# Feed-forward stages: every piece of modulation rows at the end of its group

## The reference

```python
def ada_chunks(s, w, b, k):
    mod = s @ w[:, :k * D_MODEL] + b[:k * D_MODEL]
    return [m[:, None, :] for m in jnp.split(mod, k, axis=-1)]

def swiglu(h, w_gate, w_up, w_down):
    return (jax.nn.silu(h @ w_gate) * (h @ w_up)) @ w_down

h = x + g2 * swiglu(rms_norm(x) * (1 + sc2) + sh2, ...)   # in outline, layer by layer
```

## Time and profile before

| | |
|---|---|
| runs (us) | 2203.38, 2204.43, 2203.44; median 2203.44 |
| profiled execution | 2204.52 us, of which the span from the first to the last instruction is 2202.7 us |
| mean granted TensorE clock | 0.996 |
| busy | PE 2156.7, DVE 1847.5, ACT 1327.0, POOL 112.2 us |
| stage 0 of the feed-forward stages | from 201.75 us to about 397 us |
| stage 1 | from 531 to 725 us |
| stage 2 | from 857 to 1052 us |

### The profile page before, as it was taken

One profiled execution on the slowest core, in us unless ns is written; L12 is line 12 of the kernel. 1 busy time (PEld: TensorE's weight loads), 2 busy tenths in 40 slices (PEclk: granted clock), 3 DMA queues, 4 the chain that ended last, 5 costly groups with the idle time before them and its releaser, 6 DMA issues.

```text
span 2202.7 us, 31747 instructions
## 1 busy us (share of the span) xinstructions
PE 2156.7 (98%) x12960; PEld 1899.7 (86%) x12960; DVE 1847.5 (84%) x2321; ACT 1327.0 (60%) x1495; POOL 112.2 (5%) x155
## 2 busy tenths in 40 slices
PE   6999999999999999999999999999999999999998
PEld 4888999889999979999888888888888888888886
DVE  7967888876998677888896988989897988989896
ACT  3574433575343776434633777777777777777775
POOL 3000111000010000100000000000000000000021
PEclk9999999999999999999999999999999999999999
DMA  9855988625887616885643899999998999999992
GB/s 370 299 190 201 344 314 316 230 77 211 305 299 276 225 39 239 325 325 179 227 171 136 325 372 370 365 345 363 370 358 343 369 365 371 368 345 357 373 360 85
DMA packets 137360, 633.30 MB, mean 288 GB/s; under 512 B 9304, under 2 KB 21625, under 8 KB 115194
## 3 DMA queue, kind: packets, MB, share of 16 engines
q1 hardware_dynamic: 112698, 536.83, 64.9%
q0 software_dynamic: 24512, 94.38, 11.4%
HBM read 630.13 MB, written 1.05 MB: 287 GB/s over the span
## 4 chain that ended last, share of the span: by engine, by line
PE 82%; DVE 12%; DMA 3%; issue 2%; ACT 1%; SPq 0%; DVEq 0%; ACTq 0%
PE ps L1266 80%; DVE wring_rounded L3211 3%; DMA aring<-in_ada_rows 3%; DVE aring L3238 2%; DVE work L3211 1%; PE ps L2391 1%; DVE OT L3235 1%; PE ps L1469 1%; DVE F L3218 1%; DVE F L3211 0%; PE ps L1444 0%; DVE work L3750 0%; ACT scr_rounded L2472 0%; ACT F_rounded L2472 0%; DVE work_rounded L3211 0%
## 5 line engine op out<-in xcount | busy, mean ns | idle before, releaser
L3211 DVE TENSOR_TENSOR wring_rounded<-wring,scr_rounded 128x2048 fp32r<-128x2048 f32 (+1 forms) x314 | 569.6, 1845 | 58.2 <-ACT scr_rounded L2472 57.8
L2472 ACT ACTIVATE scr_rounded<-wring 128x2048 fp32r<-128x2048 f32 (+1 forms) x314 | 479.7, 1553 | 181.8 <-PE ps L1266 125.3
L1266 PE MATMUL ps<-wring_rounded,OT_rounded 128*128 128x512 f32 (+1 forms) x1184 | 314.8, 390 | 2.6 <-DVE wring_rounded L3211 1.7
L1266 PEld LDWEIGHTS ps<-wring_rounded,OT_rounded 128*128 128x128 f32 x1184 | 220.1, 188 | 47.2 <-DVE wring_rounded L3211 2.3
L3238 DVE CUSTOM_DVE_ANT_0 aring<-aring,F,vec 128x1024 f32<-128x1024 f32 x152 | 187.9, 1283 | 35.6 <-DMA aring<-in_ada_rows 34.8
L3211 DVE TENSOR_TENSOR wring_rounded<-wring,H_rounded 128x2048 fp32r<-128x2048 f32 (+1 forms) x85 | 193.9, 2281 | 24.2 <-ACT H_rounded L2472 24.0
L3211 DVE TENSOR_TENSOR wring_rounded<-wring,aring_rounded 128x2048 fp32r<-128x2048 f32 x84 | 193.4, 2302 | 12.4 <-ACT aring_rounded L2472 12.1
L2472 ACT ACTIVATE H_rounded<-wring 128x2048 fp32r<-128x2048 f32 (+1 forms) x85 | 162.3, 1910 | 54.7 <-issue 38.4
L2472 ACT ACTIVATE aring_rounded<-wring 128x2048 fp32r<-128x2048 f32 x84 | 161.2, 1919 | 54.4 <-PE ps L1266 54.4
L1266 PE MATMUL ps<-V_rounded,wring_rounded 128*128 128x256 f32 x1184 | 177.9, 285 | 4.6 <-DVE wring_rounded L3211 4.6
L1266 PE MATMUL ps<-work_rounded,F_rounded 128*128 128x256 f32 x1056 | 169.8, 283 | 0.0
(11 more groups left out here) (391 smaller groups left out, 3695.8 us busy)
## 6 DMA issues: line engine op xcount, KB each, us to landing
wring<-in_moe_gate SPq DMA_DIRECT2D x56, 2048.0 KB, 8.5
wring<-in_moe_up SPq DMA_DIRECT2D x56, 2048.0 KB, 9.0
wring<-in_moe_down SPq DMA_DIRECT2D x56, 2048.0 KB, 8.6
aring<-in_ada_rows POOLq DMA_DIRECT2D x88, 1024.0 KB, 7.5
wring<-in_ffn_w_gate SPq DMA_DIRECT2D x10, 2048.0 KB, 11.0
wring<-in_ffn_w_up SPq DMA_DIRECT2D x10, 2048.0 KB, 15.3
wring<-in_ffn_w_down SPq DMA_DIRECT2D x10, 2048.0 KB, 10.5
wring<-in_diff_w_in SPq DMA_DIRECT2D x6, 2048.0 KB, 15.3
```

The lines of the kernel that those rows point to most:

```text
L1266: return pe.matmul(dst, lhsT, rhs, start=start, stop=stop, **kw)
L2472: return act.activation(dst, src, ACT.Copy, **kw)
L3211: return ve.tensor_tensor(dst, x, y, op)
```

## The change

In VectorE's group the conditional piece between the gate remainders and the down remainder is taken out, and all of the group's pieces are made at its end, behind the remainders of weights and activations. The number of pieces of every group, and their order among themselves, stay.

```diff
                 for n in range(FG):
                     if n + 1 < FG:
                         ff_lower_parts(f, L, n + 1, "g")
-                    if PIECES[f][n] == 3:
-                        piece()
                     ve.wait_ge(down_upper_made, FG * f + n + 1)
                     tt(down_weights(L, n), down_weights(L, n, False), down_upper(n).bitcast(F32),
                        ALU.subtract).then_inc(down_lower_made, 1)
@@
-                    for _ in range(min(PIECES[f][n], 2)):
+                    for _ in range(PIECES[f][n]):
                         piece()
```

## The result

The changed kernel takes **2210.77 us** (median of 8 runs, 2209.41 to 2212.36), the kernel before 2203.57 us on the same chip (8 runs, 2203.21 to 2205.24): a ratio of 1.003, 95% interval 1.0021 to 1.0039. It is slower by 7.2 us. The forecast was 2214.6 us, slower by 11.2: right in direction and mechanism; three of its terms were too large, and it missed a fourth.

A forecast was written before the change was run, and what follows sets the result against it. The prediction took the kernel to be bound by TensorE's matmuls. Stage 0 7.2, stage 1 2.0, stage 2 0 and clock 2.0 sum to +11.2 us on 2203.4: 2214.6 us, range 2201 to 2223.

The forecast's parts named there:

- What bounds the kernel: Whole kernel: bound by its matmuls, TensorE busy 98% of the span; time moves only where TensorE waits or stops waiting.
- part 2: Groups with three pieces in a row: VectorE needs 13.26 us plus a refill, against TensorE's 17.28 us a group.
- L: Refill time of the third piece's buffer, from GpSimd's issue to use of the rows; read as 5.46 to 10.98 us.
- part 1: Stage 0: up-remainder waits and a wait at 273.90 us can go, gaining 4.3 us at most.
- part 3: Stage 0, groups 4 to 7: four refills sum to 30.6 us, pair 9 effectively starts at 364.1 us, +7.2 us.
- part 6: Lower clock behind the last late pair of a stage: 0 to 2.0 us a stage, 2.0 us taken once.
- part 4: Stage 1, three moved groups at the median refill: pair 10 starts at 704.5 us instead of 702.57, +2.0 us.
- part 5: Stage 2: two moved pieces stand alone and could bear a refill of 12.8 us, so 0.
- The signs: Timeline: third pieces wait 3 to 8 us; TensorE waits for first gate remainders of pairs 6 to 9 in stage 0.
- The lead covers it: Rival: refills get shorter, stage 0 comes out even at 5.9 us each; 2202 to 2207 us, chance 0.20.
- Order is what hurt: Rival: the up remainder is free, 4.3 us come back, nothing new is late; 2199.1 us, chance 0.05.
- Every third refill is a slow one: Rival: weight loads and rows collide each time, clock falls in both stages; 2222 to 2230 us, chance 0.13.

The follow-up runs named there:

- The buffer experiments: Third ring buffer in stage 0 against the kernel before: old order 2200.86 us, with stage 0's five pieces moved 2200.42 us; before 2203.21 us.
- the runs above: Kernels moving only stage 1's three pieces (2205.69 us) or only stage 2's two (2204.28 us), against the kernel before, 2203.59 us.
- the kernel with stage 1 alone: Only the three pieces of stage 1 (groups 6 to 8) moved, against the kernel before: 2205.69 us against 2203.59, ratio 1.001.
- the kernel with stage 0 alone: Only the five pieces of stage 0 (groups 3 to 7) moved, against the kernel before: 2208.51 us against 2203.59, ratio 1.0023.
- the kernels with stage 2 and stage 1 alone: Only stage 2's two pieces moved, 2204.28 us; only stage 1's three moved, 2205.69 us; each against the kernel before, 2203.59 us.
- groups 6 and 7 of stage 1: Only these two groups' pieces moved, group 8 as before, against the kernel before: 2205.26 us against 2203.59, ratio 1.0007.
- three buffers: Third ring buffer for the rows in stage 0, old order, against the kernel before: 2200.86 us against 2203.21, ratio 0.9987.
- groups 3 and 5: Two buffers, only the pieces of stage 0's groups 3 and 5 moved, against the kernel before: 2202.42 us against 2203.21, ratio 0.9994.
- new counts: Three buffers and moved pieces in stage 0, stage 1 counts 1,2,2,2,2,3,3,3,3,2,1, against the kernel before: 2199.71 us against 2203.21.

## Why the prediction was right, and where it was off

*What bounds the kernel; the group's length (part 2).* Right. The formula of 13.26 us + L for a group can be read back from after: groups 4 to 7 take 22.22, 18.52, 21.03 and 18.45 us, and less the refills of 9.05, 5.34, 7.84 and 5.26 us that leaves 13.2 each time. The buffer experiments show that L is the cause, not only that it fits.

*The gain (part 1).* Real, but smaller than the bound of 4.3 us. In after the waits of the earlier trace rows at 309.55 and 310.69 us are gone and the shift falls to -1.95 us at 313 us before the late gate remainders turn it round. Some 1.5 us of this fall is the lower clock of before, which the runs above show to be no steady cost. The gain was inside the sum, so it made no error there. But the sum is measured from the 356.90 us of an execution that had lost these 1.5 us. From one that had not, it would have come out 1.5 us higher and farther from the result; that it did not is luck.

*Stage 0 (part 3).* The mechanism and the place were right, the size was not: the refills summed to 27.5 us and not 30.6, because the two beside weight loads took 9.05 and 7.84 us and not 10.2 and 9.51. The late gate remainders put pair 9 at 360.06 + 0.96 = 361.0 us, 4.1 us later than before; forecast was 7.2. Two refills of one execution were a thin sample for four others, and both were taken from the slow side. The mean of the three rows, 8.65 us, would have been worse; the measured mean of the four is 6.9. Their alternation, slow beside the weight loads and short in the gap, came out as said. The estimate from the Trainium skill ("DMA: Bandwidth & Descriptors", "Anatomy of one DMA"), 4.4 us for 1 MB, was reached by no refill here: the shortest in after took 5.26 us.

*The clock (part 6).* Right in kind for this execution, half in size. Pair 9 started at 362.10 us, 1.1 us later than its remainders allow; forecast was 2.0. Windows of after: us; PE, PEld, DVE, ACT, POOL busy; PEclk, DMA share, GB/s.

```profile
340.00:345.00 5.00, 2.15 (x9) 1.91 (x9) 5.00 (x7) 0.00 (x0) 0.72 (x1) 0.71 0.75 261
...
345.00:350.00 5.00, 5.00 (x30) 5.00 (x29) 5.00 (x6) 0.63 (x1) 0.00 (x0) 0.61 0.36 146
```

From pair 8 to pair 9 go 23.18 us. Less 17.28, and less the 3.01 us by which the gate remainders of pair 8 came late (3.97 - 0.96), that leaves 2.89 us for the lower clock. But pair 9 would have waited 1.8 us for its own remainders (361.0 against 338.92 + 17.28 + 3.01 = 359.2), so only 1.1 show. (At full clock pair 8 would have waited for its second half too, as pair 7 did; then it is 1.2 us that pair 9 would have waited, and 1.1 show all the same.) The part rests on one fall of the clock behind one wait, though: in two other executions the clock stayed full behind nearly the same wait. The prediction had said that such a loss is hidden while VectorE sets the pace; it had not used that for the last late pair, where a part is hidden too.

*Stage 1 (part 4).* The loss at pair 10 was 0.8 us (forecast 2.0): of the three refills the two last were short, 5.33 and 5.46 us, and the first long. **What failed** is a term put at nothing: that behind the late groups those with two pieces have lead again, and that what comes behind is "a chain over TensorE that only shifts". The first holds in stage 0, where three such groups follow and the shift stays at 5.2 us. In stage 1 only two groups follow, with two pieces and one, and then VectorE must hand over the remainders of the mix weights and the residual. The prediction looked for the last late *pair* and stopped there; the stage's end was the second consumer of the same lead. It cost 1.8 us here and 1.9 in the kernel with stage 1 alone.

*Stage 2 (part 5).* Right: third pieces wait 8.88 and 7.39 us, and pair 7 keeps its place.

*The sum.* Forecast 7.2 + 2.0 + 0 + 2.0 = 11.2; found in the traces 4.1 + 0.8 + 1.8 + 0 + 1.1 of clock = 7.8. Two terms too high by 3.1 and 1.2, the clock by 0.9, and a missing one of 1.8. The errors have opposite signs: that the sum is off by 3.4 us and not by more is luck.

*The signs.* Third pieces wait 5.4 us on average (over 3.5), groups 4 to 7 take 18.45 to 22.22 us (18.7 to 24 said), and what stage 0 lost is not found again behind it. TensorE waits for the gate remainders of pairs 6, 7 and 8; pair 9 comes too late itself, by the clock, to wait.

*The rivals.* "The lead covers it" needed four refills of 5.9 us each; two of four were longer. Part of it was in the result, though: refills were somewhat shorter than those read in before. "Order is what hurt" fell with the third buffer, where old and new order are equal. "Every third refill is a slow one" fell: of the four in stage 0 two were, and of all ten of after six took 7.8 us or more.

## What to carry to other kernels

Before putting consumers of a ring in an unbroken row, count them against its buffers: the work that stood between them was what hid the refill, and a row one longer than the ring waits a full transfer less the work of the consumers between, however early the engine comes to it. Such a wait is paid from the engine's lead, so ask how long the lead is, how many such rows follow each other, and which consumers come behind them, the stage's end included. Where a buffer of that size is idle, try the deeper ring first: here it gained 2.4 us with the old order, and made the order indifferent.

## What the runs showed of the hardware

**Refill times depend on company.** 1 MB of rows for a third piece took, from GpSimd's issue to its use, 5.3 to 5.5 us where next to no weights were moving and 7.8 to 9.1 us beside 2 MB loads from SyncE (stage 0 of after); the longest third refill, in stage 2, was issued at 912.66 us for the piece at 923.66: 11.0 us. The short end hardly varies, the long end does.

**Stretches of lower clock move about.** In the earlier trace rows one stands at 311 us. In after it stands at 342 us, in the kernel with stage 0 alone at 305 us, each time at a wait of TensorE of 1.3 to 2.9 us; waits of 1.16 and 1.18 us at the place of the earlier trace rows, in the kernels with stage 2 and stage 1 alone, had none. But a stretch of the same kind stands between 1200 and 1210 us, far behind all edits, in four kernels (groups 6 and 7 of stage 1; three buffers; groups 3 and 5; new counts) and not in the other traces. The same code there, first with the new counts, then before, in 5 us each (the new counts run 5.1 us ahead):

```profile
1202.00:1207.00 5.00, 5.00 (x25) 5.00 (x25) 3.79 (x6) 4.06 (x7) 0.00 (x0) 0.50 0.01 3
```

```profile
1207.00:1212.00 5.00, 5.00 (x38) 4.60 (x38) 4.96 (x8) 4.94 (x8) 0.00 (x0) 1.00 0.00 0
```

A granted clock of 0.50, the level of 1.2 GHz, with TensorE busy throughout; it costs some 2 us. Why it falls there in one execution and not in another stays open. It means that a single trace can be wrong by 2 us about a kernel, and that gains of that size must be read from medians of several runs.
